# The five norm totals of a three-layer transformer kernel: one plain f32 product against two fp32r products

## The reference, cut to what matters

```python
def rmsnorm(x, g):
    xf = x.astype(jnp.float32)
    y = xf * lax.rsqrt(jnp.mean(xf * xf, axis=-1, keepdims=True) + EPS)
    return (y * g.astype(jnp.float32)).astype(x.dtype)

def conv_ffn(h, w_up, conv_w, conv_b, w_down):
    u = h @ w_up
    u = lax.conv_general_dilated(...) + conv_b
    gate, val = jnp.split(u, 2, axis=-1)
    return (jax.nn.silu(gate) * val) @ w_down

def swiglu(x, w_gate, w_up, w_down):
    return (jax.nn.silu(x @ w_gate) * (x @ w_up)) @ w_down
```

## Time and profile before

| what | value |
|---|---|
| median of 3 runs | 2073.8 us (2073.06 to 2075.55) |
| span of the profiled execution, first to last instruction | 2071.9 us |
| TensorE busy | 2053.3 us, 99% of the span |
| VectorE busy | 1284.7 us, 62% |
| ScalarE busy | 963.9 us, 47% |
| TensorE products at L1969 | 10 records for 5 totals, 592 ns each in the middle |
| granted TensorE clock | 0.999 over the span |

### The profile page before, as it was taken

One profiled execution on the slowest core, in us unless ns is written; L12 is line 12 of the kernel. 1 busy time (PEld: TensorE's weight loads), 2 busy tenths in 40 slices (PEclk: granted clock), 3 DMA queues, 4 the chain that ended last, 5 costly groups with the idle time before them and its releaser, 6 DMA issues.

```text
span 2071.9 us, 29799 instructions
## 1 busy us (share of the span) xinstructions
PE 2053.3 (99%) x11018; PEld 1725.7 (83%) x11018; DVE 1284.7 (62%) x2111; ACT 963.9 (47%) x1883; POOL 39.1 (2%) x86
## 2 busy tenths in 40 slices
PE   8999999999999999999999999999999999999999
PEld 8999788888889788888888888888889878888887
DVE  7655688547756977774577554344548985544542
ACT  7655465334446865543344433223344664322331
POOL 0000001000000000000000000000001100000000
PEclk9999999999999999999999999999999999999999
DMA  6212233333333111333333333333332123333332
GB/s 220 68 43 61 66 99 97 97 97 97 97 89 103 34 36 61 98 97 97 97 97 97 97 97 97 97 97 97 97 94 76 36 78 96 97 97 97 97 101 86
DMA packets 101809, 185.51 MB, mean 90 GB/s; under 512 B 11552, under 2 KB 15008, under 8 KB 101408
## 3 DMA queue, kind: packets, MB, share of 16 engines
q1 hardware_dynamic: 101664, 183.61, 29.7%
HBM read 181.47 MB, written 2.10 MB: 89 GB/s over the span
## 4 chain that ended last, share of the span: by engine, by line
PE 94%; ACT 2%; DVE 2%; issue 1%; DMA 0%; SPq 0%; DVEq 0%; ACTq 0%
PE PSA L1926 25%; PE PSA L1928 25%; PE PSA L1927 25%; PE PSA L1944 3%; PE PSA L1945 3%; PE PSA L1946 3%; PE PSA L2032 2%; PE PSA L2058 2%; PE PSA L2044 2%; PE PSA L1986 1%; DVE RS L2089 1%; ACT PP L2457 1%; PE PSA L2015 0%; PE PSA L2068 0%; PE PSA L2025 0%
## 5 line engine op out<-in xcount | busy, mean ns | idle before, releaser
L2387 ACT ACTIVATE WH<-RAW 128x512 fp32r<-128x512 f32 (+2 forms) x681 | 426.6, 627 | 796.1 <-PE PSA L1928 681.8
L2101 DVE TENSOR_TENSOR WL<-RAW,WH 128x512 fp32r<-128x512 f32 (+2 forms) x681 | 467.3, 688 | 391.2 <-ACT WH L2387 366.9
L1926 PE MATMUL PSA<-HNh,WH 128*128 128x512 f32 x1440 | 562.5, 391 | 0.0
L1928 PE MATMUL PSA<-HNh,WL 128*128 128x512 f32 x1440 | 560.3, 389 | 0.0
L1927 PE MATMUL PSA<-HNl,WH 128*128 128x512 f32 x1440 | 560.2, 389 | 0.0
L1927 PEld LDWEIGHTS PSA<-HNl,WH 128*128 128x128 f32 x1440 | 270.3, 188 | 57.2 <-issue 1.2
L1926 PEld LDWEIGHTS PSA<-HNh,WH 128*128 128x128 f32 x1440 | 270.3, 188 | 56.9 <-issue 1.2
L1928 PEld LDWEIGHTS PSA<-HNh,WL 128*128 128x128 f32 x1440 | 270.3, 188 | 56.3
L1926 PE MATMUL PSA<-Gh,WH 128*128 128x512 f32 x704 | 273.9, 389 | 0.0
L1927 PE MATMUL PSA<-Gl,WH 128*128 128x512 f32 x704 | 273.9, 389 | 0.0
L1928 PE MATMUL PSA<-Gh,WL 128*128 128x512 f32 x704 | 273.9, 389 | 0.0
(11 more groups left out here) (267 smaller groups left out, 2211.5 us busy)
## 6 DMA issues: line engine op xcount, KB each, us to landing
RAW<-in_w SPq DMA_DIRECT2D x659, 256.0 KB, 2.6
XT<-in_x SPq DMA_DIRECT2D x8, 256.0 KB, 4.4
MT<-in_mem SPq DMA_DIRECT2D x2, 1024.0 KB, 5.8
out_x<-XT SPq DMA_DIRECT2D x8, 256.0 KB, 2.0
RAW<-in_w SPq DMA_DIRECT2D x8, 208.0 KB, 2.3
RAW<-in_w SPq DMA_DIRECT2D x6, 192.0 KB, 2.3
RAW<-in_w SPq DMA_DIRECT2D x8, 134.0 KB, 4.0
PAR<-in_par SPq DMA_DIRECT2D x1, 207.0 KB, 3.2
```

Of the source, the lines that this page charges most:

```text
L1926: pe.matmul(out, wh, xh, start=(a["start"] and c == 0), stop=False)
L1928: p = pe.matmul(out, wl, xh, start=False, stop=ends)
L2101: dve.tensor_tensor(l, r, h, ALU.subtract).then_inc(done.sem("split.dve"), 1)
L2387: act.activation(h, r, ACT.Copy).then_inc(done.sem("split.act"), 1)
```

## The change

The sum of squares is split like everything else: ScalarE copies `ACC` to fp32r (step "sumhigh"), VectorE subtracts (step "sumlow"), and TensorE runs two fp32r products with ones into the same bank in place of the one f32 product. The two new buffers `SUM0` and `SUM1` lie on the same memory as `SQ0` and `SQ1` and are handed out by the same `Slots`. Ones in fp32r (`ONER`) are made once by GpSimd. The planner's tables of costs are not touched; it sees five steps more on ScalarE and on VectorE, a product of another type, and other waits.

```diff
         QR = sb("QR", [128, 5, 16])
-        sb("FILL", [128, 512 - 16 - 136 - 128 - 16 - 32 - 80])
+        ONER = sb("ONER", [128, 2], F32R)
+        sb("FILL", [128, -nc.sbuf_base % 2048 // 4])
...
+        SUM = [early.enter_context(nc.sbuf_tensor(f"SUM{i}", [128, T], F32R)) for i in range(2)]
...
                     need(self.all_fed())
+                    keys = [("sum", self.name, x) for x in range(2)]
+                    for key in keys:
+                        sq.take(key, [("total.pe", self.name)])
+                    h, l = (SUM[sq.of[key]][:, 0:self.N] for key in keys)
+                    step("sumhigh", self.name, norm=self, h=h, before=sq.before[keys[0]])
+                    step("sumlow", self.name, norm=self, h=h, l=l, before=sq.before[keys[1]])
                     aux = aux_bank(("total", self.name), [("total.act", self.name)])
-                    step("total", self.name, norm=self, bank=aux)
+                    step("total", self.name, norm=self, bank=aux, h=h, l=l)
...
                 elif k == "total":
                     nm = a["norm"]
-                    w.wait_ge(s_one, 1)
+                    w.wait_ge(s_one, 2)
                     for t in psum.before["total", key]:
                         w.wait_ge(*done(*t))
-                    w.wait_ge(*done(*nm.fed(nm.adds[-1])))
-                    pe.matmul(PS[a["bank"]][:, 0:nm.N], ONES, nm.acc, start=True, stop=True).then_inc(done.sem("total.pe"), 1)
+                    w.wait_ge(*done("sumhigh.act", key))
+                    w.wait_ge(*done("sumlow.dve", key))
+                    out, ones = PS[a["bank"]][:, 0:nm.N], ONER[:, 0:1].broadcast_to([128, 128])
+                    pe.matmul(out, ones, a["h"], start=True, stop=False)
+                    pe.matmul(out, ones, a["l"], start=False, stop=True).then_inc(done.sem("total.pe"), 1)
...
+                elif k == "sumlow":
...
+                    w.wait_ge(*done("sumhigh.act", key))
+                    dve.tensor_tensor(a["l"], nm.acc, a["h"], ALU.subtract).then_inc(done.sem("sumlow.dve"), 1)
...
+                elif k == "sumhigh":
...
+                    w.wait_ge(*done(*nm.fed(nm.adds[-1])))
+                    act.activation(a["h"], nm.acc, ACT.Copy).then_inc(done.sem("sumhigh.act"), 1)
...
+            w.wait_ge(s_one, 1)
+            pool.tensor_copy(ONER[:, :], ONE[:, :]).then_inc(s_one, 1)
```

More of the change, by code:

```diff
@@ L502 @@
     "feed": ("feed.dve",),
+    "sumhigh": ("sumhigh.act",),
+    "sumlow": ("sumlow.dve",),
     "total": ("total.pe", "total.act"),
@@ L617, in program @@
         RS = [sb(f"RS{i}", [128, T]) for i in range(2)]
+        early = ExitStack()
+        SUM = [early.enter_context(nc.sbuf_tensor(f"SUM{i}", [128, T], F32R)) for i in range(2)]
+        early.close()
         SQ = [sb(f"SQ{i}", [128, T]) for i in range(2)]
@@ L2119, in vector @@
                         dve.tensor_tensor(nm.acc, nm.acc, S[:, 0:nm.N], ALU.add).then_inc(done.sem("feed.dve"), 1)
+                elif k == "sumlow":
+                    nm = a["norm"]
+                    for t in a["before"]:
+                        w.wait_ge(*done(*t))
+                    w.wait_ge(*done(*nm.fed(nm.adds[-1])))
+                    w.wait_ge(*done("sumhigh.act", key))
+                    dve.tensor_tensor(a["l"], nm.acc, a["h"], ALU.subtract).then_inc(done.sem("sumlow.dve"), 1)
                 elif k == "scale":
```

## The result

The changed kernel takes 2090.25 us (median of 5 runs, 2089.44 to 2090.81) where the kernel before takes 2073.8 (5 runs beside it, 2073.06 to 2075.78). The ratio is 1.0076, with a 95% interval of 1.0065 to 1.0086. So it is 16.4 us slower, where 2.3 us less was forecast; it lies far outside the range. The span of the profiled execution grew from 2071.9 to 2088.5 us, at a granted clock of 1.0 (2.4 GHz).

The account below looks back on a forecast made before the run. TensorE was taken to bound the kernel, busy 2053.3 of 2071.9 us. Savings at the totals of 1.23 + 0.84 + 0.25 = 2.3 us, added work hidden, took 2073.8 to 2071.5 us, range 2069.9 to 2073.6.

Parts of the forecast that it names:

- What is added, and what hides it: Five copies on ScalarE (3.2 us) and five subtractions on VectorE (3.5 us) hide in idle time; GpSimd's ones cast is free.
- the price of the ones: At each total, two fp32r products with ones take 0.45 us (bounds 0.45 to 1.72) instead of 0.86 for f32.
- first, third, fifth: Totals that stay where they are: each goes from 0.86 to 0.45 us, together 1.23 us off.
- second: Total two moves 5.4 us later, behind one more group; its wait on additions goes: 1.29 to 0.45, 0.84 us off.
- fourth: Total four moves one tile, 0.68 us; a wait of about 0.25 us (bounds 0 and 0.9) appears; 0.25 us off.
- The moved second total: Behind total two the logarithm comes 4.6 us later; the split into buffer 3 keeps 1.9 us of room; cost nothing.
- rival 3: The gain is given back later, in attention's waits for VectorE and ScalarE; 2073.8 us if all lost; chance 0.06.
- Rival 1: TensorE starves behind the moved second total, waiting for VectorE's splits; 2076.9 or 2082 us; chance 0.05.
- rival 2: At the five totals, fp32r ones are no cheaper than f32; a pair costs 1.72 us; 2077.8 us; chance 0.03.

Follow-up runs that it names:

- the second kernel: Kernel before with a longer filler, so ACC and every tensor behind it lie 32 bytes further, no instruction changed: 2091.01 us, ratio 1.0083.
- the change with the old places: The whole change with FILL sized so that ACC and all tensors behind it lie where the kernel before had them: 2073.22 us, ratio 0.9991.
- the second run of that kernel: Repeat, unaltered, of the whole change with ACC and all tensors behind it where the kernel before had them: 2073.35 us, ratio 0.9993.
- the 64-byte row: Kernel before with Gh and Gl alone 64 bytes past a multiple of 2048: 2080.42 us, ratio 1.0027.
- The second variant of the other distances: Kernel before padded so HNh, HNl, Gh, Gl lie 384, 448, 480, 160 bytes past the weights modulo 512: 2100.89 us, ratio 1.0129.

## Why the prediction was wrong

**The step that failed is the edit of `FILL` and `ONER`, a term put at nothing without a reason.** The step "What is added, and what hides it" counted what each new instruction does and left an edit out that adds none: of memory the prediction says nothing at all, though the diff showed that line. So it took every fp32r product of before to keep its 0.227 us, and those of `Gh` and `Gl` went to 0.233. Its range was bounded by the waits and the price of the ones. The edit should have had a term, and rows of before would have bounded it badly: no row there has the two operands at another distance. What would have shown that a term was missing is the list of addresses of the two kernels, side by side. The runs put 17.0 us in its place (2091.01 - 2074.02, the second kernel). By the starts it is 704 tiles x 20 ns = 14.1, and 2.8 in the stages with `AOH` and `AOL`, 16.9.

**The terms that the sum had were right, nearly to the tenth.** Read on both sides of each total, in the change with the old places, as a shift against the kernel before:

| total | forecast off, us | measured off, us |
|---|---|---|
| first, third, fifth | 0.41 each | 0.40, 0.40, 0.4 |
| second | 0.84 | 0.82 |
| fourth | 0.25 | 0.21 |
| sum | 2.3 | 2.2 |

The fp32r ones cost what any fp32r product costs: two starts 0.23 apart. The moved second total starved nobody. In the second run of that kernel the split's low part into buffer 3 ends at 844.37 + 0.64 = 845.0, 3.9 us behind the total's start at 841.1; the forecast had 843.2 and 839.3, 3.9 as well. At the fourth total the new wait is 0.13 us, inside its bounds of 0 and 0.9, and 0.12 shorter than forecast; the slower step inside the pair took most of that back. So this term came out nearly right in part by luck.

The working of the range doesn't close. The terms give at most 2.55 us off, not 3.2. And with nothing kept, 2073.8, and 0.5 to 0.8 us of spread, the upper end is 2074.3 to 2074.6, not 2073.6, which even leaves rival 3 out. The result lies outside either range.

**But of the 2.2 us only 0.7 to 0.8 show in the medians of that kernel.** Two things lie between. First, 0.36 us is lost again at 774 us, where TensorE waits for `YK` of the second attention; VectorE and TensorE in the timeline of the change with the old places:

```profile
770.31 0.69 DVE L2279 TENSOR_TENSOR XT<-PSA,XT 128x512 f32<-128x512 f32 x1 [0.26 <-issue]
...
774.50 0.64 PE L2001 MATMUL PSA<-CONST,YK 128*96 128x128 f32 x4 [0.45 <-DVE YK L2191]
```

This wait, 0.37 to 0.45 us long, stands in all five traces with the change, and in none of the ten without it. This is rival 3, with a sixth of its size. Most of it is in the first row: VectorE stands 0.26 us before this operation (0.255 to 0.258 in all five traces), for nothing that the profile shows, and its list up to `YK` carries that on to TensorE. In the ten others it doesn't stand there; the kernel before has

```profile
768.75 0.69 DVE L2257 TENSOR_TENSOR XT<-PSA,XT 128x512 f32<-128x512 f32 x1
```

The order of the operations around it is the same on TensorE, VectorE and ScalarE. What VectorE does in these 0.26 us I have not found. Second, the granted clock. Behind a wait of 2.15 us for `PP`, narrow products run in part at 1.2 GHz (granted clock 0.50 from 702 to 704 us in both profiles of the change with the old places); that stretch in the second run of the change with the old places (the clock is the third number from the end):

```profile
697.00:705.00 8.00, 6.69 (x43) 6.07 (x44) 6.31 (x15) 4.86 (x17) 0.62 (x1) 0.64 0.00 0
```

The kernel before has 0.79 there. In the two profiles of the change with old places it is 0.58 and 0.64, which costs them 1.35 and 1.3 us; in those of two variants of before that are as fast as before it is 0.63 and 1.00. So it differs from run to run, and each run's own record gives its mean clock to three digits. Among runs of equal recorded clock (coarse groups, since a step of 0.001 is 2.1 us of 2072):

| granted clock | before, us (67 runs) | change, old places (22 runs) | less |
|---|---|---|---|
| 0.998 | 2075.41 (25) | 2073.53 (12) | 1.88 |
| 0.999 | 2074.01 (23) | 2072.20 (5) | 1.81 |
| 1.000 | 2073.05 (19) | 2071.09 (5) | 1.96 |

(Medians, with the number of runs; all four groups together for the kernel before.) About 1.9 us is what 2.2 - 0.36 leaves. The means over all runs, 2074.32 and 2072.73, differ by 1.6. Counted the same way a pair costs (2082.72 - 2073.53)/20 = 0.46 us at 0.998, the same at 1.000, and an f32 total 0.87 and 0.89: what was read from starts, 0.45 and 0.86. Whether the change makes the low clock more frequent (12 of 22 runs against 25 of 67) or whether that is chance stays open; most of the difference between 1.9 us and the 0.7 of the medians hangs on it.

**The rivals.** Rival 1 (TensorE starves behind the moved total) and rival 2 (the ones no cheaper) are refuted by the rows above; rival 3 holds for 0.36 us. None of them was the cause of the loss, and the chance of 0.05 for slower had only the first two in it.

**The best candidate** is the change with the tensors in their old places: 2073.2 and 2073.4 us against 2074.0, ratios of 0.9991 (to 1.0) and 0.9993 (to 1.0002). By the medians it can't be told from no change; at equal clocks it is 1.9 us, 0.09%, faster. The forecast for the change of the totals alone, 2071.5 in a range to 2073.6, holds 2073.2 and 2073.4, both near its upper end.

## What to carry to other kernels

When a diff adds a buffer, list the address of every operand of TensorE in both kernels before counting instructions: a tensor of 8 bytes cost over 7 times what the change was worth (17.0 us against 2.2). Keep the moving operand and the weights at the same place modulo 512 bytes (the only distance tried at which no product lost anything), and compute a filler from the aligned end of what stands before it. And where a profile shows more busy time at the same count of instructions, compare distances from start to start by operand, not by line: one line here held both the slow and the unchanged products.

## What the runs showed of the hardware

**The distance in memory between the moving operand and the weights costs TensorE time.** For fp32r products of 128 x 512 with a new 128 x 128 weight each, 680 ns for three become 687, 693.5 or 700. Of the distances tried, 32 bytes either way for both parts cost most; nothing is lost when all move together. The distance modulo 512 alone doesn't foretell the cost of one product, as the 64-byte row shows (231.7, 229.2 and 225.9 ns). That it is the weights loaded *meanwhile*, and not the product's own, was argued from how loads overlap products, and no run tells the two apart. The Trainium skill, page "TensorE: Matmul & The Clock Gate", section "Step-by-step: what each phase is for", says that streamed operand and weights have two independent read ports and that loading the next weights takes no bandwidth from the running product. By that rule the place of one against the other should not matter; here it does, 2091.01 us against 2074.02 for a shift of 32 bytes alone, whatever the mechanism is.

**The same distance makes another form a little faster.** Where the activation is the stationary operand and `WH` moves (128 x 256), three products took 361 ns in the mean with the weights moved by 32 bytes against 369 before (351 against 360 in the middle). Over 448 tiles it is 3.5 us, too little to pay for the other (1440 + 704) x 20 ns = 42.9.

**Records' lengths are a poor measure of it.** In the variant with all moved by 32 bytes the row of `HNh,WH` reads 391 ns, in the change 389, with the same 680 ns from tile to tile. The second variant of the other distances has 392 for `Gh,WH` at 693.7 ns, the change 395 at 700.0. The starts are what counts.
